# Where the split weights, the loaded chunks and the activation area begin in SBUF, in a 14-phase fp32r transformer kernel

## Chip, cores and metric

One NeuronCore of a Trainium2 chip runs the whole program. The metric is the device time of one execution in microseconds (us); the time of a kernel is the median of its runs.

## What is computed

Two stacks of two layers each, on a sequence of 256 positions of width 1024, all in float32. Each layer is a feed-forward block, a mixing block and another feed-forward block, with RMS norms ahead of each. Cut to what matters:

```python
def swiglu(x, w_in, w_out):                      # D_MODEL 1024, D_FF 2816
    a, b = jnp.split(x @ w_in, 2, axis=-1)
    return (jax.nn.silu(a) * b) @ w_out

for l in range(2):                               # first stack (A)
    x = x + 0.5 * swiglu(rmsnorm(x, ffn1_norm[l]), w_ffn1_in[l], w_ffn1_out[l])
    u = rmsnorm(x, mix_norm[l])
    # u @ w_in, then latent attention, a gated recurrence in chunks of 64,
    # and attention over a memory of 256 positions; gated sum, @ w_out
    x = x + merged @ w_out[l]
    x = x + 0.5 * swiglu(rmsnorm(x, ffn2_norm[l]), w_ffn2_in[l], w_ffn2_out[l])
x = rmsnorm(x, final_norm)
for l in range(2):                               # second stack (B)
    x = x + 0.5 * swiglu_2(rms_norm(x, ffn1_norm[l]), ...)
    # h @ w_in, RWKV-7 delta rule on 8 heads of 64, chunkwise retention on 4 heads, @ w_out
    x = x + mixed @ w_out[l]
    x = x + 0.5 * swiglu_2(rms_norm(x, ffn2_norm[l]), ...)
x = rms_norm(x, final_norm)
```

## The kernel before, in words

**Activations** lie transposed: width on the 128 partitions, the 256 positions along the free axis, so a tile of x is 128 x 256 float32, which is 1024 bytes of each partition. x itself is `sb_x` (8 tiles). Nearly everything else lies in one large area of SBUF, the tensor `arena`, cut into 136 places of 1024 bytes (`area(k, at, ...)` puts a tensor at `k.arena + 4 * at`, where `at` is a multiple of T = 256 for the tiles that the large products read). Places 120 to 135 hold the normed x as the products need it: `k.xh`, its value rounded to float32r, and `k.xl`, the rest that the rounding left, 8 tiles each. The hidden tiles of a feed-forward block lie in places 0 to 43 in the same two parts.

**Weights** come from HBM as one stream of chunks, in the order of their use. A chunk is 16 blocks of 128 x 128 float32, one DMA of 1 MB issued by SP (`load_chunk`, L391 is the line of `dma_start` in `Queue.dma`), into one of three slots `sb_raw0..2` of 8192 bytes per partition. Half a chunk, a piece of 8 blocks, is split: ScalarE copies it to float32r (`split_hi`, L306, into one of four slots `sb_whi0..3`), VectorE subtracts that from the raw piece (`split_lo`, L310, into `sb_wlo0..3`). A slot has 4096 bytes per partition, a block in it 512 bytes. The splitting runs up to four pieces ahead of the products. SP loads chunk c + 3 once the lows of chunk c are done.

**Products** are made of three float32r matmuls a block (`gemm`), each with its own weight load:

```python
        pe.run(matmul(out, wh, xh, start=start and i == 0, stop=False))
        pe.run(matmul(out, wh, xl, start=False, stop=False))
        end = matmul(out, wl, xh, start=False, stop=stop and last)
```

The stationary operand (`wh`, `wl`) is one block of a split slot, 128 x 128; the moving one is one 128 x 256 tile of the area. In the profile they read `bank<-area,sb_whi` and `bank<-area,sb_wlo` (L297; MATMUL on PE, LDWEIGHTS on PEld). Where a result is wanted the other way round (`gemm_rows`), a slice of the area is stationary and four blocks of a slot (128 x 512) move: `bank<-sb_whi,area`, `bank<-sb_wlo,area`. The small products of norms, attention, recurrence and retention work in plain float32, which the profile shows as two passes a matmul, or as transposes (L301).

**Order.** The program is written out by hand, engine by engine (`Queue`); every wait is a semaphore count. The 14 phases of the profiled execution, by the start of their first product: feed-forward (11 us), mixing A0 (211), feed-forward (498, 685), mixing A1 (870), feed-forward (1155, 1344), mixing B0 (1521), feed-forward (1715, 1902), mixing B1 (2087), feed-forward (2281) and the two final norms, one at 1340 and one at the end. A feed-forward block has 528 blocks of weights, 1584 matmuls.

**Places in SBUF before.** `sb_x` and the smaller tensors are allocated from the low end, behind a scratch of 16384 bytes for dynamic DMAs; then `sb_raw0..2`, `sb_whi0..3` and `sb_wlo0..3` one behind the other (`sbuf` in `start_weights`). The area is put at the high end, at the usable end (229,368) rounded down to 32 and less its size. `sb_x`, `sb_vecs`, `sb_c1` and the scales keep their order in both kernels.

Of the kernel before, what the change touches and what calls it, by code (L numbers as in the profile page):

```python
# [11 lines left out]
F32 = mybir.dt.float32  # L12
F32R = mybir.dt.float32r
# [3 lines left out]
T = 256  # L17
# [6 lines left out]
PIECE = 8  # L24
CHUNK_BLOCKS = 16
PER_CHUNK = CHUNK_BLOCKS // PIECE
WARM = 7
RAW_SLOTS = 3
SPLIT_SLOTS = 4
AHEAD1 = (2, (6, 2))  # L30
AHEAD2 = (4, (1, 1, 1, 1))
# [196 lines left out]
ARENA = (XH + 16) * T  # L228
# [75 lines left out]
def activation(out, a, f, **kw):  # L304

    return lambda e: e.activation(out, a, f, **kw)  # L306
# [92 lines left out]
def new_slot(k, name):  # L399

    slot = State()
    slot.sem, slot.count = k.ctx.enter_context(k.nc.semaphore(name)), 0
    return slot


def sbuf(k, name, shape, dt=F32):
    return k.ctx.enter_context(k.nc.sbuf_tensor("sb_" + name, shape, dt))


def area(k, at, *shape, dt=F32, rows=128):  # L410

    n = int(np.prod(shape))
    assert dt == U8 or at + n <= ARENA, (at, n)
    k.placed += 1
    a = k.nc.alloc_sbuf_tensor_at(f"area{k.placed}", [rows, n], dt, offset=k.arena + 4 * at)[:, :]
    if len(shape) == 1:
        return a
    names = "abcd"[:len(shape)]
    return a.rearrange(f"p ({' '.join(names)}) -> p {' '.join(names)}", **dict(zip(names, shape)))
# [26 lines left out]

def start_weights(k, stream):

    w = k.w = State()
    w.stream, w.chunks, w.pieces, w.at = stream, stream.shape[0], stream.shape[0] * PER_CHUNK, 0
    w.raw = [sbuf(k, f"raw{i}", [128, CHUNK_BLOCKS * 128]) for i in range(RAW_SLOTS)]
    w.hi = [sbuf(k, f"whi{i}", [128, PIECE * 128], F32R) for i in range(SPLIT_SLOTS)]
    w.lo = [sbuf(k, f"wlo{i}", [128, PIECE * 128], F32R) for i in range(SPLIT_SLOTS)]
    w.slots = [new_slot(k, f"raw_in{i}") for i in range(RAW_SLOTS)]
    w.loaded, w.hi_done, w.lo_done, w.used = {}, {}, {}, {}


def load_chunk(k, c):  # L460
    w = k.w
    if c >= w.chunks:
        return
    if c >= RAW_SLOTS:
        k.sp.wait(k.dve, w.lo_done[(c - RAW_SLOTS + 1) * PER_CHUNK - 1])
    n = k.sp.dma(w.slots[c % RAW_SLOTS], w.raw[c % RAW_SLOTS][:, :], w.stream[c])
    for p in range(PER_CHUNK):
        w.loaded[c * PER_CHUNK + p] = (w.slots[c % RAW_SLOTS], n)

# [10 lines left out]
def raw_piece(k, n):  # L480
    c, part = divmod(n, PER_CHUNK)
    return k.w.raw[c % RAW_SLOTS][:, part * PIECE * 128:(part + 1) * PIECE * 128]


def split_hi(k, n):
    w = k.w
    k.act.wait(*w.loaded[n])
    if n >= SPLIT_SLOTS:
        k.act.wait(k.pe, w.used[n - SPLIT_SLOTS])
    w.hi_done[n] = k.act.mark(activation(w.hi[n % SPLIT_SLOTS][:, :], raw_piece(k, n), ACT.Copy))  # L490


def split_lo(k, n):
    w = k.w
    k.dve.wait(k.act, w.hi_done[n])
    if n >= SPLIT_SLOTS:
        k.dve.wait(k.pe, w.used[n - SPLIT_SLOTS])
# [163 lines left out]
def scales(k, name, at=None):  # L661


    sc = State()
    if at is None:
        sc.ssq, sc.diag, sc.sq = (sbuf(k, f"{name}_{n}", [128, T])[:, :] for n in ("ssq", "diag", "sq"))
        sc.ms, sc.tm = (sbuf(k, f"{name}_{n}", [128, 2])[:, :] for n in ("ms", "tm"))
    else:
        sc.ssq, sc.diag, sc.sq = (area(k, at + T * i, T) for i in range(3))
        sc.ms, sc.tm = area(k, at + 3 * T, 2), area(k, at + 3 * T + 8, 2)  # L670
    sc.rs = sc.diag
    return sc
# [1047 lines left out]
def prelude2(k):  # L1720

    k.act.wait(k.pe, k.pe.count)
    k.act.wait(k.dve, k.dve.count)
    k.c2 = area(k, STATE2, NC2)
    k.c2_slot = new_slot(k, "in_c2")
    k.c2_in = k.act.dma(k.c2_slot, k.c2, k.io["c2"])
    k.lora_slot = new_slot(k, "in_lora")
# [787 lines left out]
def gains(phases):  # L2515

    names = {"f1": "ffn1_norm", "mix": "mix_norm", "f2": "ffn2_norm"}
    out = []
    for i in reversed(range(len(phases))):
        p = phases[i]  # L2520
        s = "_2" if p[0] == "B" else ""
        out.append(("final_norm" + s, None, out[-1] if out else None) if p.endswith("norm") else
                   (names[p[2:]] + s, int(p[1])))
    return out[::-1]


def warm_up(k):


    zeros = area(k, (2 * NF + 9) * T, T)  # L2530
    k.pe.wait(k.dve, k.dve.mark(memset(zeros, 0.0)))
    for i in range(WARM):
        k.pe.mark(matmul(k.bank[7][:, 0:T], zeros[:, 0:128], zeros))
# [29 lines left out]
def constants_ready(k):  # L2563

    if k.constants:
        for q in (k.pe, k.act, k.dve, k.pool):
            q.wait(*k.constants)
        k.constants = None


def store(k):
    slot = new_slot(k, "stored")
    for j in range(0, NX, 2):
        k.sp.wait(k.dve, k.x_done[j + 1])
        n = k.sp.dma(slot, k.io["out"][:, j:j + 2, :], k.x[:, j:j + 2, :])
    k.sp.wait(slot, n)


def program(nc, io, phases=PHASES):
    with ExitStack() as ctx:  # L2580
        k = State()
        k.nc, k.ctx, k.io = nc, ctx, io
        k.later, k.fillers, k.unsettled, k.units, k.emptied = deque(), deque(), None, 0, {}
        k.two, k.preloaded = None, 0
        k.sp, k.pe, k.act, k.dve, k.pool = (Queue(ctx.enter_context(nc.semaphore(f"done_{n}")))
                                            for n in ("sp", "pe", "act", "dve", "pool"))
        k.bank = [ctx.enter_context(nc.psum_tensor(f"bank{i}", [128, 512], F32)) for i in range(8)]
        k.x, k.vecs, k.c1 = sbuf(k, "x", [128, NX, T]), sbuf(k, "vecs", [128, NV]), sbuf(k, "c1", [128, NC1])
        k.sx, k.scratch = scales(k, "x"), sbuf(k, "scratch", [128, 2])[:, :]
        ctx.enter_context(nc.sbuf_tensor("arena", [128, ARENA], F32, side="right"))  # L2590
        k.arena, k.placed = nc.sbuf_usable_end // 32 * 32 - 4 * ARENA, 0
        k.xh, k.xl = (area(k, (XH + NX * i) * T, NX, T, dt=F32R) for i in range(2))
        k.x_done, k.xh_done, k.xl_done = [0] * NX, [0] * NX, [0] * NX
        g = gains(phases) + [None]
        start_weights(k, io["stream"])
        if phases[0].endswith(("f1", "f2")):
            warm_up(k)
        start(k, g[0])
        steps = []
        if any(p in ("A0mix", "A1mix") for p in phases):  # L2600
            steps = prelude1(k)
            if not phases[0].endswith(("f1", "f2")):
                constants_ready(k)
            if phases[0] not in ("A0f1", "A0f2", "A1f1"):
                for step in steps:
                    step()
                steps = []
        for i, p in enumerate(phases):
            between = {}
            if p in ("A0f1", "A0f2", "A1f1") and steps:  # L2610
                between.update({1 + j: step for j, step in enumerate(steps)})
                steps = []
            if p in ("A0f1", "A1f1") and phases[i + 1:]:
                between[14] = lambda l=int(p[1]): memory_operands(k, l)
            if p == "B0f1" or (i == 0 and p in ("B0mix", "B0f2", "B1f1", "B1mix")):
                between[2] = lambda: prelude2(k)
            if p.endswith("norm"):
                if g[i + 1] is None:
                    final(k)
            elif p in ("A0mix", "A1mix"):  # L2620
                if i == 0:
                    memory_operands(k, int(p[1]))
                mix1(k, int(p[1]), g[i + 1])
            elif p in ("B0mix", "B1mix"):
                if i == 0:
                    prelude2(k)
                mix2(k, int(p[1]), g[i + 1])
            else:
                ffn(k, g[i + 1], between, lag=i == 0)
        store(k)  # L2630
        with nc.Block() as block:
            @block.sync
            def _(e):
                k.sp.replay(e)

            @block.tensor
            def _(e):
                k.pe.replay(e)

            @block.scalar  # L2640
            def _(e):
                k.act.replay(e)

            @block.vector
            def _(e):
                k.dve.replay(e)

            @block.gpsimd
            def _(e):
                k.pool.replay(e)  # L2650
# [34 lines left out]
```

How the kernel before makes its waits and increments, by code:

```python
    def wait(self, other, count):  # L375
        if count:
            self.todo.append(lambda e: e.wait_ge(other.sem, count))
# [4 lines left out]
    def mark(self, what):  # L383
        self.count += 1
        self.todo.append(lambda e: what(e).then_inc(self.sem, 1))
        return self.count
# [1 line left out]
    def dma(self, slot, out, a):  # L388
        slot.count += 16
        self.todo.append(lambda e: e.dma_start(out, a).then_inc(slot.sem, 16))
        return slot.count
```

## Time and profile before

| | |
|---|---|
| runs | 2471.56 us median of 3 (2469.4 to 2471.77) |
| the profiled execution | 2470.84 us, its span 2469.0 us (1.8 us lie around the span) |
| instructions | 49,272, of them 20,948 MATMUL passes |
| TensorE's clock | mean granted clock 0.996 of 2.4 GHz |
| busy | PE 99%, PEld 96%, DVE 68%, ACT 52%, POOL 16% |
| weights | 383 loads, 402 MB, DMA engines 46% busy |

An engine's busy share counts the time from an instruction's start to its end. A matmul of 256 columns is shown 0.28 us long and the next one begins well before it ends, so that the pace of a stream is read from starts, or from a count over a stretch of time, and not from mean durations. The page's line `PEclk` is the clock granted to TensorE.

### The profile page before, as it was taken

The numbers are of one execution on the slowest core, as the hardware profiler recorded it, in microseconds if no ns is written. First come the engines' busy times: TensorE is split into PE (matmuls) and PEld (weight loads), VectorE is DVE, ScalarE is ACT, GpSimd is POOL, SyncE is SP. The second block draws the span as 40 slices with busy tenths as digits, with TensorE's granted clock in tenths as the row PEclk, the third lists the DMA queues.
The fourth block names the chain that finished last, engine by engine and source line by source line (L and its number), as shares of the span: only waits on it lengthen the run. The fifth ranks groups of instructions, "written<-read, shape, count | busy, mean of one in ns | idle before, by whom it ended". The sixth has DMA issues, their size and how long they took to land.

```text
span 2469.0 us, 49272 instructions
## 1 busy us (share of the span) xinstructions
PE 2440.9 (99%) x20948; PEld 2380.7 (96%) x20948; DVE 1673.3 (68%) x2315; ACT 1279.0 (52%) x1812; POOL 404.8 (16%) x357
## 2 busy tenths in 40 slices
PE   8999999999999999999999999999999999999998
PEld 8999999999999999999999999989999999999998
DVE  7765776866667657878666766866666665866664
ACT  5544656644445456565454544745444444754443
POOL 4012110300200210203003013512002003422001
PEclk9999999999999999999999999999999999999999
DMA  6555433455555544345555555403555555402553
GB/s 241 188 188 180 162 124 133 173 188 186 188 188 188 188 171 154 120 139 195 185 190 191 205 203 183 155 19 120 186 185 179 187 189 186 161 26 98 193 188 120
DMA packets 57675, 410.11 MB, mean 166 GB/s; under 512 B 6384, under 2 KB 6640, under 8 KB 8688
## 3 DMA queue, kind: packets, MB, share of 16 engines
q1 hardware_dynamic: 56592, 402.15, 45.9%
q10 hardware_dynamic: 864, 4.82, 0.5%
q8 instruction: 165, 2.70, 0.4%
q14 instruction: 54, 0.44, 0.1%
HBM read 405.89 MB, written 1.05 MB: 165 GB/s over the span
## 4 chain that ended last, share of the span: by engine, by line
PE 87%; DVE 5%; ACT 3%; issue 3%; POOL 2%; DMA 0%; DVEq 0%; SPq 0%; POOLq 0%; ACTq 0%
PE bank L297 86%; DVE sb_wlo L310 2%; ACT area L306 2%; DVE area L310 2%; DVE area L321 1%; PE bank L301 1%; ACT sb_whi L306 1%; POOL area L310 0%; ACT L306 0%; POOL sb_x_ssq L310 0%; POOL area L315 0%; POOL sb_x_sq L310 0%; DVE sb_x L321 0%; DMA sb_x<-x 0%; POOL area L334 0%
## 5 line engine op out<-in xcount | busy, mean ns | idle before, releaser
L297 PE MATMUL bank<-area,sb_whi 128*128 128x256 f32 x11752 | 2093.6, 281 | 11.0 <-DVE area L321 5.7
L297 PEld LDWEIGHTS bank<-area,sb_whi 128*128 128x128 f32 x11752 | 1799.7, 188 | 23.8 <-DVE area L321 9.6
L297 PE MATMUL bank<-area,sb_wlo 128*128 128x256 f32 x5876 | 1642.3, 279 | 4.5 <-DVE sb_wlo L310 4.4
L306 ACT ACTIVATE sb_whi<-sb_raw 128x1024 fp32r<-128x1024 f32 x762 | 801.9, 1058 | 777.0 <-PE bank L297 771.0
L297 PEld LDWEIGHTS bank<-area,sb_wlo 128*128 128x128 f32 x5876 | 1103.6, 188 | 6.4 <-DVE sb_wlo L310 6.4
L310 DVE TENSOR_TENSOR sb_wlo<-sb_raw,sb_whi 128x1024 fp32r<-128x1024 f32 x762 | 962.0, 1271 | 163.2 <-ACT sb_whi L306 161.8
L310 DVE TENSOR_TENSOR area<-area,area 128x256 f32<-128x256 f32 (+7 forms) x502 | 259.7, 526 | 248.4 <-ACT area L306 245.7
L306 ACT ACTIVATE area<-area 128x256 f32<-128x256 f32 (+6 forms) x515 | 252.1, 498 | 83.9 <-DVE area L310 59.1
L310 DVE TENSOR_TENSOR area<-bank,sb_x_diag 128x512 f32<-128x512 f32 x244 | 167.3, 686 | 36.2 <-PE bank L297 21.6
L297 PE MATMUL bank<-area,area 128*64 128x64 f32 (+5 forms) x2304 | 181.4, 254 | 2.1 <-ACT area L306 1.9
L310 POOL TENSOR_TENSOR sb_x_ssq<-sb_x 128x256 f32<-128x256 f32 x12 | 13.1, 1088 | 1014.9 <-DVE sb_x L321 883.0
L297 PEld LDWEIGHTS bank<-area,area 128*64 128x64 f32 (+2 forms) x2304 | 157.8, 157 | 21.2 <-ACT area L306 7.7
L306 ACT ACTIVATE area<-bank 64x512 f32<-64x512 f32 (+5 forms) x174 | 88.0, 514 | 153.1 <-PE bank L301 112.3
L310 DVE TENSOR_TENSOR area<-bank,area 128x512 f32<-128x512 f32 (+5 forms) x204 | 105.1, 543 | 81.3 <-PE bank L297 44.2
L310 POOL TENSOR_TENSOR sb_x_sq<-sb_x 128x256 f32<-128x256 f32 x84 | 102.0, 1214 | 232.4 <-DVE sb_x L321 228.9
L321 DVE SCALAR_TENSOR_TENSOR sb_x<-bank,sb_x 128x256 f32<-128x256 f32 x96 | 39.5, 422 | 138.6 <-PE bank L297 138.6
L310 POOL TENSOR_TENSOR area<-area 128x512 f32<-128x512 f32 (+1 forms) x66 | 73.3, 1111 | 352.6 <-DVE area L310 177.6
L306 ACT ACTIVATE area<-sb_x,sb_vecs 128x256 fp32r<-128x256 f32 (+1 forms) x96 | 47.0, 506 | 76.1 <-DVE sb_x L321 73.2
L310 POOL TENSOR_TENSOR sb_x_ssq<-sb_x_ssq,sb_x_sq 128x256 f32<-128x256 f32 x87 | 79.7, 916 | 26.3 <-ACT sb_x_sq L306 19.7
L321 DVE SCALAR_TENSOR_TENSOR area<-sb_x,sb_vecs,area 128x256 fp32r<-128x256 f32 x88 | 70.3, 814 | 10.1 <-ACT area L306 10.1
L310 POOL TENSOR_TENSOR area<-area,area 128x256 f32<-128x256 f32 (+2 forms) x36 | 53.8, 1507 | 93.4 <-ACT area L306 36.0
L297 PE MATMUL bank<-sb_whi,area 128*128 128x512 f32 x208 | 66.6, 401 | 1.0 <-ACT area L306 0.6
(82 smaller groups left out, 705.7 us busy)
## 6 DMA issues: line engine op xcount, KB each, us to landing
sb_raw<-stream SPq DMA_DIRECT2D x379, 1024.0 KB, 4.8
sb_raw<-stream SPq DMA_DIRECT2D x4, 512.0 KB, 6.9
area<-lora ACTq DMA_DIRECT2D x2, 768.0 KB, 4.5
area<-c ACTq DMA_DIRECT2D x1, 1504.0 KB, 7.2
sb_x<-x SPq DMA_DIRECT2D x4, 256.0 KB, 5.0
area<-mem ACTq DMA_DIRECT2D x1, 1024.0 KB, 8.2
out<-sb_x SPq DMA_DIRECT2D x4, 256.0 KB, 2.9
area<-m ACTq DMA_DIRECT2D x1, 512.0 KB, 5.8
```

The source lines that it names most:

```text
L297: return lambda e: e.matmul(out, lhsT, rhs, start=start, stop=stop, skip_group_check=True, tile_position=at)
L301: return lambda e: e.transpose(out, a, ident)
L306: return lambda e: e.activation(out, a, f, **kw)
L310: return lambda e: e.tensor_tensor(out, a, b, op)
L321: return lambda e: e.scalar_tensor_tensor(out, a, s, b, op0, op1)
```

## The change

No instruction, no wait and no order changes; the programs have the same instructions on each engine, and only addresses differ. A new function `place` computes them from the high end of SBUF:

- the area begins at a multiple of 1024 bytes (`ROW`);
- all eight split slots lie under it, high and low of a slot side by side, each 64 bytes (`LINE`) below a multiple of 1024;
- the three raw slots lie under those;
- one tensor `placed` reserves the range from the lowest raw slot to the end;
- the scratch for dynamic DMAs shrinks from 16384 to 1024 bytes, and everything allocated from the low end moves down by 15,360 bytes, which is 15 times 1024.

```diff
+ROW = 4 * T
+LINE = 64
...
+def place(k, end):
+    k.arena = (end - 4 * ARENA) // ROW * ROW
+    at, k.split_at = k.arena, {}
+    for i in range(SPLIT_SLOTS):
+        for part in range(2):
+            at -= 4 * PIECE * 128
+            k.split_at[part, i] = at - LINE
+    at -= LINE
+    k.raw_at = []
+    for i in range(RAW_SLOTS):
+        at -= 4 * CHUNK_BLOCKS * 128
+        k.raw_at.append(at // 32 * 32)
+    return k.raw_at[-1]
...
 def start_weights(k, stream):
-    w.raw = [sbuf(k, f"raw{i}", [128, CHUNK_BLOCKS * 128]) for i in range(RAW_SLOTS)]
-    w.hi = [sbuf(k, f"whi{i}", [128, PIECE * 128], F32R) for i in range(SPLIT_SLOTS)]
-    w.lo = [sbuf(k, f"wlo{i}", [128, PIECE * 128], F32R) for i in range(SPLIT_SLOTS)]
+    nc, piece, chunk = k.nc, [128, PIECE * 128], [128, CHUNK_BLOCKS * 128]
+    w.hi, w.lo = ([nc.alloc_sbuf_tensor_at(f"sb_{name}{i}", piece, F32R, offset=k.split_at[part, i])
+                   for i in range(SPLIT_SLOTS)] for part, name in enumerate(("whi", "wlo")))
+    w.raw = [nc.alloc_sbuf_tensor_at(f"sb_raw{i}", chunk, F32, offset=k.raw_at[i]) for i in range(RAW_SLOTS)]
...
 def program(nc, io, phases=PHASES):
-        ctx.enter_context(nc.sbuf_tensor("arena", [128, ARENA], F32, side="right"))
-        k.arena, k.placed = nc.sbuf_usable_end // 32 * 32 - 4 * ARENA, 0
+        k.placed = 0
+        low = place(k, nc.sbuf_usable_end // 32 * 32)
+        ctx.enter_context(nc.sbuf_tensor("placed", [128, (nc.sbuf_usable_end - low) // 32 * 8], F32, side="right"))
...
 def kernel(**inputs):
-    nc = bacc.Bacc("TRN2", target_bir_lowering=False, num_devices=1)
+    nc = bacc.Bacc("TRN2", target_bir_lowering=False, num_devices=1, dynamic_dma_scratch_size=1024)
```

The addresses that come out, in bytes of a partition, and what they leave when divided by 1024 (each slot of a kind leaves the same, since their sizes are multiples of 1024):

| | before | leaves | after | leaves |
|---|---|---|---|---|
| large area | 90,080 | 992 | 89,088 | 0 |
| `sb_whi0`, even blocks | 56,480 | 160 | 84,928 | 960 |
| `sb_whi0`, odd blocks | 56,992 | 672 | 85,440 | 448 |
| `sb_wlo0`, even blocks | 72,864 | 160 | 80,832 | 960 |
| `sb_raw0` | 31,904 | 160 | 48,064 | 960 |
| `sb_x` | 16,512 | 128 | 1,152 | 128 |

The moving tile so begins 832 bytes past the stationary block before (modulo 1024), or 320 for an odd block; after the change it is 64, or 576.

## Rows read from the trace of the kernel before

**Rows 1.** The page: PE's busy time and, in 40 slices, its granted clock.

```profile
PE 2440.9 (99%) x20948; PEld 2380.7 (96%) x20948; DVE 1673.3 (68%) x2315; ACT 1279.0 (52%) x1812; POOL 404.8 (16%) x357
...
PEclk9999999999999999999999999999999999999999
```

**Rows 2.** The page: the chain that ended last, by engine.

```profile
PE 87%; DVE 5%; ACT 3%; issue 3%; POOL 2%; DMA 0%; DVEq 0%; SPq 0%; POOLq 0%; ACTq 0%
```

**Rows 3.** The page's costliest groups: form xcount | busy us, mean ns | idle before <-releaser.

```profile
L297 PE MATMUL bank<-area,sb_whi 128*128 128x256 f32 x11752 | 2093.6, 281 | 11.0 <-DVE area L321 5.7
...
L297 PE MATMUL bank<-area,sb_wlo 128*128 128x256 f32 x5876 | 1642.3, 279 | 4.5 <-DVE sb_wlo L310 4.4
```

**Rows 4.** Busy time by stretch: 150 us in each of two feed-forward blocks.

```profile
core 0: us, PE busy (x) PEld busy (x) DVE busy (x) ACT busy (x) POOL busy (x), PEclk, DMA share, GB/s
1160.00:1310.00 150.00, 150.00 (x1276) 150.00 (x1275) 98.46 (x127) 72.58 (x103) 9.20 (x10) 1.00 0.53 188
1360.00:1510.00 150.00, 150.00 (x1325) 150.00 (x1325) 100.83 (x129) 73.34 (x100) 14.63 (x12) 1.00 0.55 198
```

**Rows 5.** Timeline of PE at 1200 us: start us, us, engine line op out<-in xcount.

```profile
1200.17 0.28 PE L297 MATMUL bank<-area,sb_wlo 128*128 128x256 f32 x1
...
1201.94 0.28 PE L297 MATMUL bank<-area,sb_wlo 128*128 128x256 f32 x1
```

**Rows 6.** Timeline of PE at 1400 us.

```profile
1400.07 0.28 PE L297 MATMUL bank<-area,sb_wlo 128*128 128x256 f32 x1
...
1401.77 0.28 PE L297 MATMUL bank<-area,sb_wlo 128*128 128x256 f32 x1
```

**Rows 7.** Timeline of PE around four norm sums at 1151.7 us.

```profile
1151.25 0.28 PE L297 MATMUL bank<-area,sb_wlo 128*128 128x256 f32 x1
...
1151.59 0.28 PE L297 MATMUL bank<-area,sb_wlo 128*128 128x256 f32 x1
1151.71 0.50 PE L297 MATMUL bank<-sb_c,sb_x_ssq 128*128 128x2 f32 x4
...
1152.39 0.28 PE L297 MATMUL bank<-area,sb_wlo 128*128 128x256 f32 x1
...
1152.74 0.28 PE L297 MATMUL bank<-area,sb_wlo 128*128 128x256 f32 x1
```

**Rows 8.** Busy time by stretch: two whole feed-forward blocks.

```profile
498.00:682.00 184.00, 184.00 (x1563) 183.95 (x1563) 118.73 (x147) 88.10 (x119) 17.20 (x15) 1.00 0.52 185
...
1344.00:1521.00 177.00, 177.00 (x1564) 176.97 (x1563) 120.91 (x156) 86.69 (x119) 17.28 (x15) 1.00 0.57 201
```

**Rows 9.** Busy time by stretch: four short ones.

```profile
19.40:24.80 5.40, 5.40 (x50) 5.40 (x49) 1.76 (x2) 2.12 (x2) 1.13 (x1) 1.00 0.90 276
332.30:337.30 5.00, 5.00 (x46) 5.00 (x46) 3.63 (x6) 3.85 (x8) 2.35 (x2) 1.00 0.43 180
999.00:1004.00 5.00, 5.00 (x47) 5.00 (x46) 3.65 (x6) 4.20 (x9) 2.59 (x2) 1.00 0.43 180
...
2156.00:2166.00 10.00, 10.00 (x91) 10.00 (x90) 8.28 (x12) 7.78 (x10) 4.73 (x3) 1.00 0.44 155
```

**Rows 10.** Groups of PE in mixing A0, 212 to 495 us.

```profile
L297 PE MATMUL bank<-area,sb_whi 128*128 128x256 f32 x1170 | 210.5, 282 | 0.5 <-DVE area L310 0.2 <-DVE area L321 0.2
```

**Rows 11.** Groups of PE in mixing B0, 1521 to 1712 us.

```profile
L297 PE MATMUL bank<-area,sb_whi 128*128 128x256 f32 x481 | 90.2, 287 | 2.9 <-DVE area L321 2.5 <-ACT area L306 0.3
```

**Rows 12.** Timeline of PE where the split weights move, 226 us.

```profile
226.44 0.63 PE L297 MATMUL bank<-sb_whi,area 128*128 128x512 f32 x2
...
227.84 0.63 PE L297 MATMUL bank<-sb_whi,area 128*128 128x512 f32 x2
```

**Rows 13.** Timeline of the weight loads of norm sums at 1339.8 us.

```profile
1339.83 0.53 PEld L297 LDWEIGHTS bank<-sb_c,area 128*128 128x128 f32 x4
1340.28 0.30 PEld L297 LDWEIGHTS bank<-area,sb_whi 128*128 128x128 f32 x2
```

**Rows 14.** The page: DMA issues, xcount, KB each, median us to landing.

```profile
sb_raw<-stream SPq DMA_DIRECT2D x379, 1024.0 KB, 4.8
```

## The prediction

> **What bounds the kernel now.** I read the page first: PE is busy 99% of the span at a granted clock of 0.9 or more in every slice [rows 1], and the chain that ended last is PE's for 87% [rows 2]. Two groups carry it: 11,752 matmuls with `sb_whi` as weights and 5,876 with `sb_wlo`, 17,628 in all, with idle time of 11.0 and 4.5 us before them [rows 3]. So time is the number of these matmuls times the distance from one start to the next, and only that distance can move much. The mean duration of 281 ns says nothing of it, since the matmuls overlap; I read it from counts and starts.
>
> The busy time by stretch gives the surprise. Two stretches of 150 us, each inside a feed-forward block of the same shapes with PE never idle, show 1276 and 1325 matmuls [rows 4]. Less two that are counted because they only reach in over an edge, this is 117.7 ns and 113.4 ns a matmul. The timelines say the same: five triples (two highs, one low) take 1.77 us at 1200 us, 118 ns each [rows 5], and 1.70 us at 1400 us, 113.3 ns each [rows 6]. The granted clock is 1.00 in both, the 2.4 GHz level [rows 4], so this is not the clock. It is not VectorE or ScalarE: they do as much in the quick stretch (DVE 100.8 against 98.5 us, ACT 73.3 against 72.6) [rows 4]. **The stream has two paces at the same addresses modulo 1024.** A whole block takes 177 us at the one and over 184 us at the other, for the same 1563 matmuls or so [rows 8]. The pace stays until something else comes between: before four norm sums at 1151.7 us a triple takes 0.34 us, after them 0.35 us [rows 7]. The quick pace is rare: one block (1558 matmuls between its interruptions) and six short pieces, four of them in [rows 9], one before the sums of [rows 7] (27 matmuls) and one of 14 at 2275 us; 1,833 of 17,628, a tenth.
>
> At 2.4 GHz, 256 columns need 106.7 ns. The slow pace is 11 ns over that, the quick one 6.7. Something that depends on how two activities lie to each other in time costs PE a little in each matmul. While one matmul streams its tile out of SBUF, the next block of weights is loaded, also out of SBUF: PEld is busy all 150 of 150 us [rows 4]. These two are my suspects, and where in SBUF the one reads while the other reads elsewhere is just what the change sets, for each of the 17,628.
>
> **The change, part by part.** No instruction is added, removed or moved on any engine, nor past a queue, so no wait comes or goes by itself.
>
> *Split slots and area.* Before, a moving tile begins 832 (even blocks) or 320 bytes (odd) past the block of weights modulo 1024; after, 64 or 576. Area starts were 32 off a multiple of 64 bytes, and so were the slots; now both are on one. No row shows the new relation, so I bound it. The best end: weight loads alone. Four of them, for norm sums whose matmuls are two columns long, take 1340.28 - 1339.83 = 0.45 us, 112 ns each [rows 13]; the stream can't run faster than its loads, so at best 117.7 - 112 = 5.7 ns a matmul in the slow parts. The worst end: the stream in which 512 columns of split weights move runs at (227.84 - 226.44) / 6 = 233 ns [rows 12], 20 ns over the 213 ns of its columns; were that much lost in each matmul of 256 columns, the pace would be 127 ns, 9 ns slower than now. Between them I take the value of the nearest rows, the quick pace: **4.4 ns off each slow matmul**. My reason is that it exists in this kernel, in the same loop, and holds for 177 us once reached [rows 8], while the new relation alters just the overlap on which the two paces must differ.
>
> Feed-forward: 8 blocks of 1584 matmuls; seven are slow, 7 x 1584 x 4.4 ns = 48.8 us. All of it counts, as PE is never idle there: the slow block has 184.00 busy of 184.00 [rows 8].
>
> Mixing A: 1170 highs and half as many lows, 1755 [rows 10], and two such stages, 3510, less some 120 already quick. The idle time before them is 0.5 us [rows 10], so nearly all is on the path; I count 0.9: 3390 x 4.4 x 0.9 = 13.4 us.
>
> Mixing B: 481 x 1.5 = 722 [rows 11], two stages, 1443, less some 110. Here VectorE and ScalarE chains of the recurrence end more of the waits (2.9 us before the highs, most by DVE) [rows 11] and a quicker filler only waits for them longer. I count half: 1330 x 4.4 x 0.5 = 2.9 us.
>
> The 312 matmuls with 512 moving columns may gain too; at most their 20 ns, 6.2 us. I take nothing and keep it for the low end. The float32 passes are set by loads at 112 ns [rows 13], and I take nothing.
>
> *What is late next.* At the quick pace DVE is busy 101 of 150 us, ACT 73, the DMA engines 55% [rows 4]. A chunk lasts 48 x 113.3 ns = 5.4 us, a load lands 4.8 us after its issue [rows 14] with three slots in turn. All have room, and the quick block shows them keeping up [rows 8].
>
> *Raw slots, `sb_x`, smaller scratch.* The splits read and write places that leave the same remainder as each other, before (160) and after (960); `sb_x` keeps its 128. Loads now write to multiples of 64. Both are covered by the slack just named. If a load were late by a whole landing time, 4.8 us a chunk, the kernel would slow at once by hundreds of us; nothing points to it, as every load of the program is issued by SP or ScalarE and none by POOL. The Trainium skill (SBUF — State Buffer, "SBUF size: 192, 224, or 256?") says that scratch holds the rings of descriptors that software writes. By that rule a smaller one costs nothing here; the trace agrees in so far as its queues are all of the kinds "hardware dynamic" and "instruction".
>
> **The sum**: 48.8 + 13.4 + 2.9 = 65.1 us. The profiled execution took 2470.84 us (span 2469.0 and 1.8 around it), 0.7 below the median of the runs, 2471.56. 2470.84 - 65.1 = 2405.7; I say **2406 us**.
>
> **The rule that speaks against it.** The rows show a stream that is slower than its columns need, by two different amounts [rows 4 to 6]. The Trainium skill (TensorE: Matmul & The Clock Gate, "Step-by-step: what each phase is for") says that TensorE has one SBUF read port for the moving operand and another for weight loads, and that loading the next tile doesn't steal bandwidth from the running matmul. By that rule addresses can't matter. The same page ("Back-to-back issue gap") gives 256 columns 256/2.4 + 2.5 = 109.2 ns; an estimate by it for all 17,628, in place of their mean of 117.3 (a tenth quick), would be 143 us less, about 2328 us, but no row shows the stream below 113 ns.
>
> **The rivals.**
>
> *No effect of addresses.* The cost comes from something in PE's own timing (how the start of a load falls against the start of a matmul), and the two paces at one set of addresses speak for it: address alone plainly doesn't decide. Even and odd blocks, 512 bytes apart in relation, run alike, so that I can't see a dependence on it within the stream: the evenly spaced triples span both kinds [rows 5]. That is the strongest point against me. Then the time stays at 2471, with some blocks changing pace by chance; a block is 1584 x 4.4 = 7 us, so chance could also bring 2464 or 2478. 0.20.
>
> *The quick state is lost or a slower one found (slower).* If a collision between moving tile and weight block now falls early in each matmul, 64 bytes apart at the start, every stretch might lock into the slow pace. Place: the block at 1344 us and the six short pieces. Price: 1833 x 4.4 ns = 8 us, 2479 us. It decides once over some 1,100 of the 1,833 have gone (4.9 us, 0.2%). A third, slower pace is the worse form: each 1 ns more costs 17.6 us, up to the 127 ns of the bound and about 2640 us. 0.16 together, 0.06 of it for the worse form.
>
> *Only part locks.* As now, but with more stretches quick, say two to five blocks of the seven: 2425 to 2466 us. 0.13.
>
> *Better than quick.* The stream reaches its loads' 112 ns: another 1.3 ns x 17,628 = 23 us, and up to 6 us of the wide matmuls: 2377 us. 0.09.
>
> **How the numbers follow.** My forecast, nearly all at the quick pace (2395 to 2425), has 0.42. Faster by over 0.2% (5 us, about what a measurement of this kernel can tell from none): 0.42 + 0.13 + 0.09 = 0.64; same 0.20; slower 0.16. The range goes from the best end, 2377, to the lost quick state with a little room, 2480; left out are the third pace and a pace under the loads', about 0.1. The likeliest case's own range is 2395 to 2425.
>
> **What would show it.** In the profile of the changed kernel, 150 us inside any feed-forward block count about 1325 matmuls, a triple takes 0.34 us everywhere, the eight blocks last 177 to 180 us each, and the clock row stays. Wrong: about 1276 and 0.353 us (no effect), fewer than 1270 (slower pace), or a new wait of ScalarE for raw chunks (loads). If the blocks are at 177 us but the sum is less, it went in the mixing stages, as idle before PE's highs.

## The result, and the profile after

The changed kernel took 2479.07 us in the median of 8 runs (2476.31 to 2481.65), the kernel before 2471.66 us beside it (8 runs, 2469.4 to 2474.74): a ratio of 1.003, 95% interval [1.002, 1.004]. It is slower by 7.4 us; I had said 65 us faster. The time is inside my range of 2377 to 2480 only because the rival of the lost quick pace was taken into it.

Busy time by stretch of the changed kernel, columns as in [rows 4]: the same two windows, then the blocks that answer to [rows 8].

```profile
1160.00:1310.00 150.00, 150.00 (x1276) 150.00 (x1276) 99.66 (x129) 73.64 (x106) 9.07 (x10) 1.00 0.52 187
1360.00:1510.00 150.00, 150.00 (x1276) 150.00 (x1275) 97.76 (x126) 71.00 (x98) 11.46 (x10) 1.00 0.53 194
...
499.00:683.00 184.00, 184.00 (x1565) 184.00 (x1563) 118.70 (x147) 88.12 (x119) 17.22 (x15) 1.00 0.53 186
...
1346.00:1530.00 184.00, 184.00 (x1563) 183.95 (x1563) 121.15 (x156) 86.83 (x119) 17.22 (x15) 1.00 0.54 194
```

The first window has 1276 matmuls in 150 us, as before; the second, too, where [rows 4] had 1325. The block that took 177 us [rows 8] takes 184. In these windows clock, VectorE, ScalarE and DMA are as they were. The slow pace itself has not moved by a tenth of a nanosecond: 117.78 ns a matmul over a stretch of 1558 in both traces, and the quick one is 113.33 where it occurs. Call a distance between the starts of two neighbours in a stream quick when it is under 115.5 ns: 1,839 were quick before and 279 after; 1,560 x 4.4 ns = 6.9 us of the 9.5 us between the two profiled spans (2469.0 and 2478.5).

Most of the rest is the clock, in stretches too short for the page's 40 slices. Here and there the granted clock is at 0.50, the 1.2 GHz level, for a few us, and the matmuls then start 213 ns apart. Two such stretches of the changed kernel have no counterpart in the trace of the kernel before:

```profile
52.80:55.80 3.00, 3.00 (x16) 3.00 (x15) 2.83 (x14) 2.25 (x4) 0.00 (x0) 0.50 0.67 227
937.10:939.80 2.70, 2.70 (x14) 2.70 (x14) 1.64 (x4) 2.69 (x3) 2.36 (x2) 0.50 0.53 222
```

In all, 63 distances of the changed kernel are near 213 ns and 42 of the kernel before, and 21 x 95.5 ns is another 2.0 us. Such stretches vary between executions and are not tied to the change: a second profile of the changed kernel (e2) has neither of the two, and PE idled about as long just ahead of 52 us in both traces (2.8 us here, 3.0 us before, where the clock stayed).

The page of the changed kernel, the parts that answer to [rows 1 to 3] and [rows 14]:

```profile
PE 2449.4 (99%) x20948; PEld 2389.2 (96%) x20948; DVE 1674.3 (68%) x2315; ACT 1278.9 (52%) x1812; POOL 406.0 (16%) x357
...
PEclk9999999999999999999999999999999999999999
...
PE 88%; DVE 5%; issue 3%; ACT 3%; POOL 1%; DMA 0%; DVEq 0%; SPq 0%; POOLq 0%; ACTq 0%
...
L299 PE MATMUL bank<-area,sb_whi 128*128 128x256 f32 x11752 | 2102.6, 281 | 12.0 <-DVE area L323 6.0
...
L299 PE MATMUL bank<-area,sb_wlo 128*128 128x256 f32 x5876 | 1648.1, 280 | 4.5 <-DVE sb_wlo L312 4.4
...
sb_raw<-stream SPq DMA_DIRECT2D x379, 1024.0 KB, 4.8
```

Everything reads as before; a page doesn't show this difference, since it shows durations (281 ns) and not distances. The block at 1346 us is entered like this. Timeline of PE in the changed kernel:

```profile
1345.39 0.59 PE L299 MATMUL bank<-sb_x_diag,sb_c 128*128 128x256 f32 x2
1345.82 0.59 PE L299 MATMUL bank<-area,sb_c 128*128 128x256 f32 x2
1346.07 0.59 PE L299 MATMUL bank<-area,sb_whi 128*128 128x256 f32 x2
...
1347.20 0.28 PE L299 MATMUL bank<-area,sb_wlo 128*128 128x256 f32 x1
...
1347.55 0.28 PE L299 MATMUL bank<-area,sb_wlo 128*128 128x256 f32 x1
```

And in the kernel before:

```profile
1343.22 0.59 PE L297 MATMUL bank<-sb_x_diag,sb_c 128*128 128x256 f32 x2
1343.65 0.59 PE L297 MATMUL bank<-area,sb_c 128*128 128x256 f32 x2
1343.89 0.58 PE L297 MATMUL bank<-area,sb_whi 128*128 128x256 f32 x2
...
1344.65 0.28 PE L297 MATMUL bank<-area,sb_wlo 128*128 128x256 f32 x1
...
1344.99 0.28 PE L297 MATMUL bank<-area,sb_wlo 128*128 128x256 f32 x1
```

The same instructions come in the same order, and then a triple takes 0.35 us in the one and 0.34 in the other, for the next 1558 matmuls. It is the one feed-forward block entered from two norms, one with its diagonal in `sb_x_diag` and one with its diagonal in the area (`bank<-area,sb_c`), a tensor that the change moved against the constants. That alone doesn't decide: the stretch of 1151 matmuls from 75 us, inside the first block, also follows a `bank<-area,sb_c` and was slow in both kernels.

### The profile page after: what moved, and what is told of

Read it like the earlier page. It is cut to its first block, busy times and chain, and to the rows that moved or that the text cites. A ratio compares the mean times of both kernels' runs of the same rounds, so it can differ in the third digit from the quotient of the medians.

```text
span 2478.5 us, 49272 instructions
## 1 busy us (share of the span) xinstructions
PE 2449.4 (99%) x20948; PEld 2389.2 (96%) x20948; DVE 1674.3 (68%) x2315; ACT 1278.9 (52%) x1812; POOL 406.0 (16%) x357
## 4 chain that ended last, share of the span: by engine, by line
PE 88%; DVE 5%; issue 3%; ACT 3%; POOL 1%; DMA 0%; DVEq 0%; SPq 0%; POOLq 0%; ACTq 0%
PE bank L299 87%; DVE sb_wlo L312 2%; ACT area L308 2%; DVE area L312 2%; DVE area L323 1%; PE bank L303 1%; ACT sb_whi L308 1%; POOL sb_x_ssq L312 0%; ACT L308 0%; POOL area L312 0%; DVE sb_x L323 0%; POOL sb_x_sq L312 0%; DMA sb_x<-x 0%; DVE area L318 0%; DVE sb_x L312 0%
## 5 line engine op out<-in xcount | busy, mean ns | idle before, releaser
L308 ACT ACTIVATE area<-bank 64x512 f32<-64x512 f32 (+5 forms) x174 | 88.0, 514 | 152.5 <-PE bank L303 111.7
```

## Experiments

### Is the pace of a stretch fixed, and does the scratch matter? (e1, e2, e3)

e1 and e2 are the two kernels again, unedited. e3 is the kernel before with one edit:

```diff
-    nc = bacc.Bacc("TRN2", target_bir_lowering=False, num_devices=1)
+    nc = bacc.Bacc("TRN2", target_bir_lowering=False, num_devices=1, dynamic_dma_scratch_size=1024)
```

> The kernel before, unchanged, profiled a second time. Theory A (which pace a stretch has is fixed by the program, its addresses and the timing that they set): the feed-forward block at 1344 us is quick again (177 us), the other seven slow (184 us), 2469 to 2475 us. Theory B (the pace of each stretch is drawn anew in every execution): another block, none or several are quick, and the time moves by 7 us for each.

> The changed kernel, unchanged, profiled a second time. Theory A: again no quick feed-forward block, one quick stretch of 169 matmuls near 472 us, 2476 to 2482 us. Theory B: quick blocks come and go here too.

> The kernel before with the small scratch alone: raw and split slots, sb_x and the rest move down by 15 times 1024 bytes, the area stays, so every relation modulo 1024 is as before. Theory 1 (the relation of tile and weight block modulo 1024 picks the pace): 2471 us, the block at 1344 us quick. Theory 2 (any change of the program draws the paces anew): other stretches are quick, 2464 to 2480 us. Theory 3 (the small scratch costs something): about 2479 us, no quick block.

Measured: e1 2469.66 us, the block near 1344 us quick again; e2 2476.34 us, no quick block; e3 2475.93 us in the median of 10 runs (2469.09 to 2480.62), a ratio of 1.0006 [0.999, 1.0022], the block quick in its profile. The window from 1360 to 1510 us, in e1, e2 and e3:

```profile
1360.00:1510.00 150.00, 150.00 (x1326) 150.00 (x1325) 100.83 (x127) 73.29 (x100) 15.78 (x13) 1.00 0.54 193
```

```profile
1360.00:1510.00 150.00, 150.00 (x1276) 150.00 (x1275) 96.89 (x123) 70.75 (x98) 13.28 (x11) 1.00 0.52 186
```

```profile
1360.00:1510.00 150.00, 150.00 (x1325) 150.00 (x1325) 100.55 (x127) 73.75 (x101) 15.47 (x13) 1.00 0.54 196
```

So theory A holds for the large blocks of a profile, but not fully: the short stretches that were quick differed from one profile to the next of the same kernel (in e2 one of 142 matmuls at 50 us, in place of the one of 169 at 472), and the runs of the kernel before beside e3 lie mostly at 2469 to 2476 us with three at 2478 to 2483, about one block's 7 us higher (these runs have no profile, so that a lost block is the likely reason and not a seen one). Places decide how likely a stretch is to lock into the quick pace, and in some stretches chance has the last word. Of e3's ten runs five lie at 2477.7 to 2480.6 us, so that its interval leaves room for up to 5 us; theory 3 in the form foretold (2479 us and no quick block) falls, and e12 below, which has the small scratch too, bounds its cost at 0.1% (ratio 1.0001 [0.9992, 1.001]).

### Which relation gives which pace? (e4, e5)

Both leave the layers out and only run streams of 48 matmuls in the triples of `gemm`, with 128 x 128 float32r blocks and 256 moving columns, at chosen places. The heart of e4:

```python
for r, (rel, width) in enumerate([(r, T) for r in RELS] + [(832, w) for w in WIDTHS]):
    at = W_AT - rel                      # tile minus block leaves rel (mod 1024)
    for e in range(16 if width == T else 4):
        for q in range(4):
            matmul(bank6[:, 2*q:2*q+2], plain[:, 0:128], plain[:, 0:2])
        matmul(bank5[:, 0:260+2*e], hi[:, 0:128], xh[:, 0:260+2*e])
        stream(hi, lo, xh, xl, width, 48)
```

> A kernel that only measures: the layers are left out. 18 relations of moving tile and weight block modulo 1024 (0, 32, 64, 96, 128, 192 and on in steps of 64 to 960), each with 16 streams of 48 matmuls of 256 columns in the triples of gemm, each stream after four passes of 2 columns and one matmul of 260 to 290 columns, two more at each entry; then 12 widths from 2 to 512 columns at the relation of before. Theory A (address): at some relations all 16 streams are at 113.3 ns, at others all at 117.8. Theory B (entry phase alone): the same few entries are quick at every relation, whatever the address. Rival C: a third pace, below 113 or above 118 ns, at some relation. Widths under 200 columns should all stand at the pace of the loads, 112 ns, if loads bound them.

> A second kernel that only measures (layers left out), built as e4. Relations 0 to 240 modulo 256 in steps of 16 and 168, 184, 200, 216, each with 6 or 8 streams of 48; then relation 192 and relation 64 with tile and weight slots shifted together by 32, 64, 96, 128 (and 224) bytes; then highs and lows of the weights at different relations (192 with 0, 0 with 192, 192 with 64), then the xl tiles 64 bytes off; then widths 240 to 512 at relations 192 and 0. Theory R (the difference modulo 256 of the moving tile and the block loaded beside it sets the pace): shifts change nothing (192: 113.3, 64: 117.8); with highs at 192 and lows at 0 only one distance of the three in a triple becomes 120, the one in which the low block is loaded beside xl; 384 columns take 6.7 ns over their 160 at relation 192 and 13.3 at 0. Rival T (absolute alignment): the pace follows the shift. A relation between the tested ones may be at the pace of the loads, 111.7.

Measured in e4, as the mean of the last 24 distances of a stream (the first stream of each relation, which follows a refill of the slots, is left out: there the granted clock was between its two levels, 0.77 from 140 to 146 us):

```
relation mod 1024        mod 256   distance, ns (15 streams each)
0, 256, 512, 768           0       119.9 to 120.0, all
32                         32      116.6 to 116.7 in 13, 117.8 in 2
64, 320, 576, 832          64      117.7 to 117.8, all
96                         96      120.0, all
128, 384, 640, 896        128      118.5 to 118.9 in 46 of the 60, 120.0 in the others
192, 448, 704, 960        192      113.3 to 113.4 in 11, 117.8 in 4, the same entries each time
```

The relation matters, with a period of **256 bytes**: at the four remainders that were run at four relations each, the paces are the same four times (at 128 only the entries that are at 120.0 differ). **Before, the tile lay 832 past the block and after the change 64, and both are 64 modulo 256.** That is why the slow pace didn't move. Only at 192 was the quick pace seen in e4, and there the entry picked it: two columns more in the one matmul ahead of a stream could decide between 113.3 and 117.8 ns. Theory A (address) and theory B (entry) were each half right.

e5 in steps of 16 found nothing under 113.3 ns (168 gave it in 4 of 5 streams, 200 and 208 none). Timelines of PE in e5, 12 triples between the rows of a pair: relation 0, relation 64, relation 192 quick and relation 192 slow, and highs at 192 with lows at 64.

```profile
37.03 0.28 PE L297 MATMUL bank<-mfill,wl_ak 128*128 128x256 f32 x1
...
41.35 0.28 PE L297 MATMUL bank<-mfill,wl_ak 128*128 128x256 f32 x1
...
263.44 0.28 PE L297 MATMUL bank<-mfill,wl_ao 128*128 128x256 f32 x1
...
267.68 0.28 PE L297 MATMUL bank<-mfill,wl_ao 128*128 128x256 f32 x1
...
729.22 0.28 PE L297 MATMUL bank<-mfill,wl_bm 128*128 128x256 f32 x1
...
733.30 0.28 PE L297 MATMUL bank<-mfill,wl_bm 128*128 128x256 f32 x1
...
735.73 0.28 PE L297 MATMUL bank<-mfill,wl_bm 128*128 128x256 f32 x1
...
739.97 0.28 PE L297 MATMUL bank<-mfill,wl_bm 128*128 128x256 f32 x1
...
1747.20 0.28 PE L297 MATMUL bank<-mfill,wl_dl 128*128 128x256 f32 x1
...
1751.28 0.28 PE L297 MATMUL bank<-mfill,wl_dl 128*128 128x256 f32 x1
```

The 36 matmuls take 4.32, 4.24, 4.08, 4.24 and 4.08 us: 120.0, 117.8, 113.3, 117.8 and 113.3 ns each. Shifting tile and block together by 32 to 128 bytes (and by 224 at relation 64) kept the set of values: 113.3 or 117.8 ns at 192, and 117.8 ns at 64 but for two streams in 35 at 113.3; which entries were quick did change with the shift, though by e5's construction the operands ahead of the stream were then elsewhere against it as well. So rival T falls for the values. Theory R missed on two counts. With highs at 192 and lows at 0 all three distances of a triple became 117 to 118 ns (in two of the seven streams 122, 127 and 118), where the theory had one of them alone at 120: the matmuls do not pay separately. The reverse pair (highs 0, lows 192) stood at 117.8 ns in all seven, and the `xl` tiles moved by 64 bytes at relation 192 gave 117.8 to 119.5. And 384 columns took 173.3 ns at relation 0 as at 832, and 173.3 to 176.7 at 192. The gain of relation 192 was seen at 256 columns only: 248 columns took 113.3 to 116.7 ns at 192, 115.0 at 0 and 113.3 at 832; 288 columns took 133.3, 131.7 and 132.2. A pair for which I had forecast no pace was the best: highs at 192 and lows at 64 gave 113.3 to 113.7 ns in 7 of 7.

The widths of e4 (relation 832) show what is paid for. At 192, 224 and 240 columns the stream stands at 111.6 to 111.8 ns, whatever the width: the loads bound it. From 248 columns up it is over what its columns take at 2.4 GHz by 10.0 ns (248), 11.1 (256), 11.7 (264), 12.2 (288), 13.3 (320 and 384) and 15.6 to 20 (512). The excess grows by only 3.3 ns while the columns from 248 to 384 take 57 ns more, so that most of it is a sum per matmul, and each matmul has one load. What it is paid for within a matmul these widths don't say.

### The relation of 192 in the kernel (e6, e7), and that of 0 (e8)

e6 is the kernel before with

```diff
+    sbuf(k, "pad", [128, 32])
     w.hi = [sbuf(k, f"whi{i}", [128, PIECE * 128], F32R) for i in range(SPLIT_SLOTS)]
```

e7 and e8 are the changed kernel with

```diff
-LINE = 64
+LINE = 192
```

and `LINE = 0`.

> The kernel before with one pad of 128 bytes ahead of the split slots and nothing else: even blocks leave 288 in place of 160, tile minus block is 704 modulo 1024, which is 192 modulo 256 where before (832) and the changed kernel (64) are both 64. Theory R: most stretches at 113.3 ns, 60 to 70 us less than before, 2400 to 2412 us. Theory B (the pace comes from the entry alone, addresses only shuffle it): 2465 to 2482 us.

> The changed kernel with LINE = 192 in place of 64, so that the slots lie 192 bytes below a multiple of 1024 (64 above a multiple of 256): relation 192 modulo 256. Theory R: as e6, 2400 to 2412 us. Rival (the aligned layout itself costs 7 us): e7 is 7 us over e6. Theory B: 2465 to 2482 us.

> The changed kernel with LINE = 0: slots and area both at multiples of 1024, relation 0. Theory R: every stretch at 120.0 ns, 2.2 ns more for each of 12,672 matmuls of the feed-forward blocks and most of the 4,950 others, 35 to 40 us over the changed kernel, 2512 to 2520 us. Theory B: 2465 to 2482 us.

Measured: e6 2459.11 us (6 runs), ratio 0.9949 [0.9935, 0.9962]; e7 2425.59 us (6 runs, 2419.92 to 2438.86), 0.9815 [0.9792, 0.9838]; e8 2511.99 us (4 runs), 1.0163 [1.0147, 1.0179]. 150 us of a feed-forward block in e7 and in e8:

```profile
500.00:650.00 150.00, 150.00 (x1326) 150.00 (x1325) 100.94 (x129) 74.19 (x103) 13.44 (x11) 1.00 0.55 192
```

```profile
520.00:670.00 150.00, 150.00 (x1253) 150.00 (x1252) 94.59 (x121) 69.59 (x97) 12.02 (x10) 1.00 0.50 183
```

(1326 - 2) in 150 us is 113.3 ns; (1253 - 2) is 119.9. In e7, 15,546 of 17,358 distances were quick and all eight blocks with them; in e8, 20. e8 came at the low end of its expectation (2512 to 2520), e7 missed its 2412 by 14 us, and e6, with the same relation, missed it by 47 us and had only 5,005 quick ones, one whole block and 1,150 matmuls of the first among them. Theory B falls, and theory R lacks a part.

### Why e6 and e7 differ, and why the change lost its block (e9, e10, e12)

```diff
-    k.arena = (end - 4 * ARENA) // ROW * ROW
+    k.arena = (end - 4 * ARENA) // ROW * ROW - 32
```

This line makes e9 of e7, and e12 of the changed kernel. e10 is e9 with a pad of 224 bytes ahead of `sb_x`.

> e7 with area, split and raw slots all 32 bytes lower (area leaves 992, slots 800), so that tile minus block stays 192 modulo 256; sb_x, the diagonal and the constants stay. These are the places modulo 256 of e6, in the layout of e7. Theory S (only the relation inside the stream counts, and e6 and e7 differ by something else of their layouts, such as the order of slots): as e7, 9 in 10 quick, 2420 to 2435 us. Theory N (the places of the norm operands, which are read just before a stream, against those of the stream decide which of the two paces of relation 192 it falls into; or the absolute place does): as e6, 3 in 10 quick, 2455 to 2466 us.

> e9 with a pad of 224 bytes ahead of sb_x, so that the norm operands too are 32 lower modulo 256: every difference between any two tensors is that of e7 modulo 256, and all absolute places are 32 off. Theory N1 (differences alone): as e7, 2420 to 2435 us. Theory N2 (the absolute place modulo 64): as e6, 2455 to 2466 us.

> The changed kernel (LINE = 64) with area, split and raw slots 32 bytes lower: the places modulo 256 of the kernel before (area 224, slots 160, norm operands as they were), in the changed layout. Theory N (either form): the block at 1344 us is quick again in most executions, 2469 to 2474 us for most and 2478 to 2482 for the rest, as before. Theory S (the layout or the order of the slots took the quick block): 2476 to 2482 us as the changed kernel.

Measured: e9 2459.28 us (4 runs, 2458.38 to 2464.16), which is e6 and not e7; e10 2434.72 us (4 runs, 2427.05 to 2450.4), quick in 13,516 of 17,356 distances, against 5,986 in e9; e12 2472.26 us (12 runs), a ratio of 1.0001 [0.9992, 1.001] to the kernel before, and its block is back:

```profile
1344.00:1521.00 177.00, 177.00 (x1564) 176.98 (x1562) 120.91 (x156) 86.59 (x119) 17.27 (x15) 1.00 0.57 201
```

So the order of the slots (theory S) makes no difference that these runs can tell. Moving area and slots by 32 bytes together, with their relation to each other kept, costs 34 us at relation 192; moving the norm operands along gives most of it back (theory N1, with a remainder of some 9 us over e7 that four runs of wide spread don't settle). What the change did to the time is these 32 bytes: it took the area, and the slots with it, to another place against `sb_x_diag` and the constants, and the block at 1344 us no longer locked into the quick pace. Take the 32 bytes back and the 7 us come back (e12). That they act through the norm operands, and not through the absolute place, is shown at relation 192 (e9 against e10); at relation 64 no run moved those operands along, and there it is carried over.

### A version that beats both (e11)

```diff
-    for i in range(SPLIT_SLOTS):
-        for part in range(2):
+    for part in range(2):
+        for i in range(SPLIT_SLOTS):
             at -= 4 * PIECE * 128
-            k.split_at[part, i] = at - LINE
-    at -= LINE
+            k.split_at[part, i] = at - (192, 320)[part]
+    at -= 320
```

> e7 with the lows at another relation: highs 192, lows 64 modulo 256 (all four high slots first, then the lows). In e5 this pair was at 113.3 to 113.7 ns in 7 of 7 streams, where 192 with 192 had 4 of 7. If that holds in the kernel: every stretch quick, 2408 to 2420 us, and a narrower spread than e7's 2420 to 2439. If it was luck of the entries: 2420 to 2460 us.

Measured: 2419.48 us (4 runs, 2418.52 to 2420.23), ratio 0.9785 [0.9771, 0.9798]. 16,847 of 17,312 distances were quick, and the runs spread by 1.7 us where e7's spread by 19. Busy time by stretch of e11, a block and then mixing A0 and B0:

```profile
500.00:650.00 150.00, 150.00 (x1326) 150.00 (x1326) 100.97 (x129) 74.29 (x103) 13.45 (x11) 1.00 0.54 192
```

```profile
1490.00:1681.00 191.00, 184.09 (x1918) 170.30 (x1917) 134.02 (x192) 107.92 (x159) 66.38 (x54) 0.99 0.28 101
207.00:487.00 280.00, 275.68 (x2187) 260.86 (x2186) 209.10 (x326) 166.17 (x243) 52.17 (x44) 1.00 0.44 156
```

And mixing A0 in the kernel before:

```profile
211.00:495.00 284.00, 281.91 (x2190) 267.65 (x2190) 209.15 (x325) 166.95 (x243) 52.34 (x44) 1.00 0.44 154
```

And mixing B0:

```profile
1521.00:1712.00 191.00, 186.24 (x1916) 172.45 (x1915) 133.58 (x191) 107.74 (x159) 65.20 (x53) 0.99 0.29 101
```

This kernel also prices my sum, since it is the case that I forecast. Between the two spans lie 2469.0 - 2417.3 = 51.7 us, not 65. A feed-forward block gave 7.0 us (498.3 to 685.7 us before, 490.2 to 670.6 in e11), as forecast; the seven slow ones gave some 46 us in all, since the first gave only 4.5: from 52.9 to 55.9 us the clock of e11 was at 0.50 and that of the kernel before was not. The mixing stages gave 3.7 and 2.1 us (A) and about nothing (B: 193.8 us before, 193.5 after, and 194.1 and 194.5), 5.7 in all where I had 16.3. Some 3 us of that shortfall too are stretches at the lower clock that the trace before lacks (15 distances near 213 ns in A1, 14 more of them in B1). In A0, which has none, the work that PE is busy with shrank by 6.2 us and its idle time grew from 2.1 to 4.3 us; in B0 it shrank by 2.2 us and the idle time took it all.

## Why the prediction was wrong, point by point

- **What bounds the kernel**: right. Two paces at one clock, lasting until an interruption, and the medians followed the paces. What I had not seen is that short falls of the clock move single executions by 1 to 4 us.
- **The two suspects**: right as far as it goes. The relation of tile and block sets the pace: 120.0, 117.8 or 113.3 ns at relations 0, 64 and 192 modulo 256 (e4, e5), and 2512, 2479 and 2426 us in the kernel (e8, changed, e7). That it is a collision between load and stream is argued: the pace depends on where the one lies against the other, and most of the excess is a sum per matmul. No run sees a port.
- **The step that failed** is "the new relation alters just the overlap on which the two paces must differ". I took 832, 320, 64 and 576 modulo 1024, because the change speaks of 1024, and called 64 new. The runs show a period of 256, and 832, 320, 64 and 576 all leave 64: the change altered nothing inside the stream. I even held the clue, that blocks 512 bytes apart run alike, and took it as a sign against addresses; it is what a period of 256 makes.
- **What I put at nothing**: I wrote that the area and the slots had lain 32 bytes off a multiple of 64 and that `sb_x` keeps its place, and gave the shift between them no price. It was the only difference modulo 256 in what the large products and the norms read, and with everything else kept it is worth 7 us at relation 64 (e12) and 34 us at 192 (e9).
- **The value of 4.4 ns off each slow matmul**: nothing came off, 117.78 ns in both. It is the right size for the kernel that does alter the relation (e7, e11). *Better than quick* found nothing either: at 256 columns no relation gave less than 113.3 ns, and the loads' 111.7 was reached only at 240 columns and fewer. In *only part locks*, two to five blocks of 7.0 us are 2436 to 2457 us; my 2425 to 2466 was wider than its own terms.
- **The slower rival** was what happened: the block at 1344 us lost, priced at 8 us and 2479 us, measured 7.4 us and 2479.07. I gave it 0.16 with the worse form. That the number fits to a tenth is luck: 1833 distances and 1,560 are not the same, and the six short pieces only changed places. Its main place was right, its reason not: the relation inside the stream was unchanged, and the loss came with the shift of stream and area against the operands ahead of it (e12; e9 and e10 at relation 192).
- **"Address alone doesn't decide"**: right, in e4 the length of one matmul ahead of a stream decides at relation 192, and nearly never at 64 (never in e4, 2 streams in 35 in e5's shifted ones).
- **Mixing stages, 16.3 us**: too much by 10.6 even when the pace does change (e11). The shares of 0.9 and 0.5 came out at about 0.4 and 0, or 0.5 and 0.2 with the clock's part taken out (an estimate): short streams between chains of VectorE and ScalarE turn a quicker PE into waiting, as in A0 and B0 above, though PE shows busy 99% over the whole.
- **Scratch, raw slots and loads cost nothing**: right within 0.1% (e12; e3's own interval is wider), and loads still land in 4.8 us.
- **The rule on two read ports**: the Trainium skill (TensorE: Matmul & The Clock Gate, "Step-by-step: what each phase is for") says that loading the next tile doesn't steal bandwidth from the running matmul. Here the same stream takes 113.3 to 120.0 ns by its places alone, so for float32r blocks with 256 moving columns the measurement decides against the conclusion that I drew from it, that addresses can't matter. The 109.2 ns that I took from the Trainium skill (the same page, "Back-to-back issue gap") are by that section the gap of an isolated matmul, not of a stream with a load for each, so that 2328 us was no estimate for this kernel.

## What to carry to other kernels

Read the distance between starts of the matmuls that bound a kernel, and in several stretches: a stream may have more than one pace, and a mean duration hides it. Where blocks of float32r weights are loaded beside moving tiles of 256 columns, place them by their difference modulo 256 bytes, and measure a few differences at the width that is used, with a kernel that does only that; one such kernel of 18 relations told more here than any argument from a trace. Before giving a chance to a change of places, compute the quantity that it is said to change under every period that might hold, and see whether it changes at all.

## What the hardware showed that I had not expected

- The pace of a float32r stream of 256 columns depends on tile minus block modulo 256: 113.3 to 120.0 ns, up to 6% of TensorE's time, the granted clock being 1.00 in all five stretches of e5 shown above.
- At one relation there can be two stable paces (113.3 and 117.8 ns, often at 192 and rarely at 64), picked within the first few matmuls after an interruption and then kept for over 1500; which one depends on where the stream lies against the operands just before (e9, e10) and on a few columns of one matmul (e4), and in some stretches varies between executions.
- Different relations for the two parts of the weights (192 and 64) made the quick pace almost certain: 97% of the distances, against 90% at 192 alone.
- In e4, streams with 2, 64 and 128 moving columns ran at a granted clock of 0.50, the 1.2 GHz level, and there the loads came 213.3 ns apart whatever the width; from 2175 to 2180 us, at 192 columns, it was 1.00 and they came 111.7 ns apart. A load's pace follows the granted clock. In the kernels themselves the clock falls to 0.50 for a few us at places that differ between executions of one kernel. Busy time by stretch of e4, at 2 and at 128 columns:

```profile
2026.00:2034.00 8.00, 8.00 (x39) 8.00 (x39) 0.00 (x0) 0.00 (x0) 0.00 (x0) 0.50 0.00 0
...
2140.00:2148.00 8.00, 8.00 (x40) 8.00 (x39) 0.00 (x0) 0.00 (x0) 0.00 (x0) 0.50 0.00 0
```
